# Single products as fillers, a top-64 split around the first dots, and picks that alternate with attention queries

## The reference, cut to what matters

```python
h = rmsnorm(x, ln1_g)
q_a, k_a, v_a, q_i, k_i, w_i, q_b, k_b, v_b, g_b = project(h, w_in)

# sparse attention: an indexer scores all keys, the top 64 (132 for the streams) are attended to
dots = einsum('bthd,bsd->bths', q_i, k_i)
score = where(allowed, einsum('bth,bths->bts', w_i, relu(dots)), -inf)
top_s, idx = lax.top_k(score, topk)
o_a = attention over the rows idx of k_a, v_a
# retention: a chunkwise recurrence with a state per head
x = x + concat([o_a, o_b]) @ w_out

# PEER: per token and head, 16 of 128 x 128 experts; an expert is one row of peer_u and one of peer_v
h = rmsnorm(x, ln2_g)
q = h @ w_query                        # 8 heads, two halves of 128
v1, i1 = top_k(q[first half] @ keys1.T, 16); v2, i2 = top_k(q[second half] @ keys2.T, 16)
cand_s = v1[:, None] + v2[None, :];  top_s, sel = top_k(cand_s, 16);  gate = softmax(top_s)
act = gelu(einsum('thkd,td->thk', peer_u[e_idx], h))
x = x + einsum('thk,thkd->td', gate * act, peer_v[e_idx])
y = rmsnorm(x, ln_final_g)
```

## Time and profile before

| | |
|---|---|
| median of 3 runs | 1145.67 us (1145.54 to 1146.6) |
| profiled execution | 1144.68 us, of which span 1142.9 us |
| PE busy | 858.6 us (75%) |
| DVE busy | 784.3 us (69%) |
| POOL busy | 539.9 us (47%) |
| ACT busy | 453.6 us (40%) |
| moved by DMA | 456.60 MB, of which the gathers' queue 402.68 MB |

### The profile page before, as it was taken

One profiled execution on the slowest core, in us unless ns is written; L12 is line 12 of the kernel. 1 busy time (PEld: TensorE's weight loads), 2 busy tenths in 40 slices (PEclk: granted clock), 3 DMA queues, 4 the chain that ended last, 5 costly groups with the idle time before them and its releaser, 6 DMA issues.

```text
span 1142.9 us, 12079 instructions
## 1 busy us (share of the span) xinstructions
PE 858.6 (75%) x3879; PEld 396.1 (35%) x3884; DVE 784.3 (69%) x2005; ACT 453.6 (40%) x1423; POOL 539.9 (47%) x437
## 2 busy tenths in 40 slices
PE   8999988997896858685586777576766675656566
PEld 6748743443232424242243342133223222211111
DVE  2325877876677778986666786757877767667544
ACT  2121444333443434543564663343343333333334
POOL 0002444553555645563553554555564555465452
PEclk9999999999998988998888998799788779887869
DMA  9902999999999999999999999999999999999996
GB/s 375 410 2 73 418 425 426 426 425 429 426 402 424 426 429 426 425 401 415 425 427 425 425 427 428 419 427 427 426 426 427 427 426 428 427 426 428 427 427 274
DMA packets 66791, 456.60 MB, mean 400 GB/s; under 512 B 8227, under 2 KB 10019, under 8 KB 15526
## 3 DMA queue, kind: packets, MB, share of 16 engines
q0 software_dynamic: 55888, 402.68, 83.8%
q1 hardware_dynamic: 10694, 52.87, 11.5%
q10 hardware_dynamic: 144, 0.26, 0.1%
HBM read 451.49 MB, written 3.24 MB: 398 GB/s over the span
## 4 chain that ended last, share of the span: by engine, by line
DMA 45%; PE 29%; DVE 13%; POOL 5%; ACT 4%; issue 4%; SPq 0%; POOLq 0%; DVEq 0%
DMA rows<-in_uv,ids 32%; PE ps L598 28%; DMA wt<-in_uv,ids 9%; DVE rows L2042 6%; POOL rows L537 2%; POOL work L520 1%; DMA rows<-in_w_qi 1%; DMA wt<-in_uv,last_ids 1%; DVE wt L2042 1%; ACT wt L1249 1%; ACT work L1249 1%; DMA wt<-in_w_q 1%; ACT wgt L1249 1%; POOL wt L537 1%; PE ps L601 1%
## 5 line engine op out<-in xcount | busy, mean ns | idle before, releaser
L537 POOL DMA_INDIRECT rows<-in_uv,ids x352 | 401.8, 1141 | 439.2 <-PE ps L598 355.4
L598 PE MATMUL ps<-rows,work 128*64 128x512 f32 x1416 | 409.1, 706 | 240.9 <-ACT work L1249 240.5
L2042 DVE CUSTOM_DVE_ANT_0 rows<-rows,wt 128x1024 f32<-128x1024 f32 x226 | 276.7, 1225 | 162.3 <-DMA rows<-in_uv,ids 161.0
L1249 ACT ACTIVATE zact<-zdot 128x1 f32<-128x1 f32 x354 | 71.4, 202 | 485.7 <-DVE zdot L2042 485.1
L598 PEld LDWEIGHTS ps<-rows,work 128*64 128x64 f32 x1416 | 95.9, 151 | 471.8 <-ACT work L1249 333.8
L598 PE MATMUL ps<-wt 128*128 128x128 f32 (+6 forms) x719 | 198.4, 484 | 31.0 <-ACT wt L1249 29.5
L2042 DVE CUSTOM_DVE_ANT_0 rows<-rows,masks 128x1024 f32<-128x1024 f32 x128 | 156.2, 1223 | 67.9 <-DMA rows<-in_uv,ids 66.9
L598 PEld LDWEIGHTS ps<-wt 128*128 128x128 f32 (+2 forms) x724 | 98.8, 188 | 111.0 <-issue 62.1
L1249 ACT ACTIVATE work<-pair,wgt 128x64 f32<-128x64 f32 x354 | 123.1, 348 | 11.6
L1249 ACT ACTIVATE wgt<-zact,gates 128x1 f32<-128x1 f32 x354 | 104.3, 295 | 11.5
L598 PEld LDWEIGHTS ps<-work,wt 128*128 128x128 f32 (+1 forms) x664 | 82.5, 198 | 50.4 <-issue 49.9
(11 more groups left out here) (178 smaller groups left out, 722.9 us busy)
## 6 DMA issues: line engine op xcount, KB each, us to landing
wt<-in_w_q SPq DMA_DIRECT2D x7, 2048.0 KB, 12.0
rows<-in_uv,ids POOLq DMA_INDIRECT x352, 14.3
rows<-in_w_out SPq DMA_DIRECT2D x2, 2048.0 KB, 32.7
wt<-in_w_out SPq DMA_DIRECT2D x2, 2048.0 KB, 12.0
wt<-in_ckv SPq DMA_DIRECT2D x16, 256.0 KB, 11.6
x<-in_x SPq DMA_DIRECT2D x5, 512.0 KB, 8.3
rows<-in_w_qi SPq DMA_DIRECT2D x1, 2048.0 KB, 13.1
wt<-in_w_qa SPq DMA_DIRECT2D x1, 2048.0 KB, 13.1
```

What stands on the lines that cost most here:

```text
L537: pool.indirect_dma_start(row[s], None, a["uv"], bass.IndirectOffsetOnAxis(ap=ids[:, own(n // KP).start + n % KP:own(n // KP).start + n % ...
L598: return nc.tensor.matmul(out, lhsT, rhs, start=start, stop=stop)
L1249: return nc.scalar.activation(*args, **kw)
L2042: V.tensor_tensor_reduce(row[s][:, 0:D], row[s][:, 0:D], h2r[t][:, n % 2, :], 1.0, 0.0, ALU.mult, ALU.add, zdots[s]).then_inc(dotted, 1)
```

## The change

- `index_queries` takes its range in single products (32 of them) and not in blocks of 8, and its calls among the opening's steps are cut finer: 3, 4 and 2 products where 8, 8 and 8 were, and 4 of tile 2 ahead of `dots_1` where 8 were; what is left of each comes later.
- The transposes of tile 0's normed tokens go in two halves (`h2_t0`), each as soon as its half of the columns is there. The wait for ACT's sum of squares moves from PE to the two copies behind the transposes.
- `spread_out(0)` goes ahead of `dots_1(3)`.
- `y_start(0)` moves from before the first add to tick 12. The first add clears its accumulator itself (start flag), and `y_start(0)` adds to it.
- The first four pairs of picks alternate with the four `later_qa` on PE; `query_scores(1)` stands ahead of them. On ACT picks 6 and 7 come ahead of the second copy.
- Of tile 1's eight rounds of top-64, DVE does four before the first dot and the others, one a tick, behind the first dots. Tile 1's attention moves back by 1 to 6 ticks.

```diff
-            index_queries(1, 6, 0, 1)
-            h2_t(0)
-            index_queries(1, 6, 1, 2)
+            h2_t0(0)
+            index_queries(1, 6, 0, 3)
+            h2_t0(1)
+            index_queries(1, 6, 3, 7)
             query(0)
-            index_queries(1, 6, 2, 3)
+            index_queries(1, 6, 7, 9)
             query_scores(0)
-            index_queries(1, 6, 3, 4)
+            index_queries(1, 6, 9, 32)
             pe.wait_ge(gb_sb, 1)
-            index_queries(2, 7, 0, 1)
+            index_queries(2, 7, 0, 4)
...
             sums_1(0)
+            spread_out(0)
             dots_1(3)
             sums_1(1)
-            spread_out(0)
             sums_1(2)
             sums_1(3)
-            index_queries(2, 7, 1, 4)
+            index_queries(2, 7, 4, 32)
             query(1)
-            later_qa(0)
             query_scores(1)
             pe.wait_ge(qi_sb, 3)
-            y_start(0)
             add_experts(0)
+            later_qa(0)
+            add_experts(2)
             later_qa(1)
-            add_experts(2)
+            add_experts(4)
             pe.wait_ge(scored, 2)
             later_qa(2)
+            add_experts(6)
             later_qa(3)
-            add_experts(4)
```

PE, the new transposes and tile 1's attention; `until` counts picks:

```diff
+            def h2_t0(e):
+                pe.wait_ge(gained, e + 1)
+                for c in range(4 * e, 4 * e + 4):
+                    last = tr(ps[:, 3 * e, (c % 4) * P:(c % 4 + 1) * P], h2[:, c * P:(c + 1) * P])
+                if e:
+                    last.then_inc(h2t_ps, 1)
...
             def attention_1():
+                yield from until(6)
                 scores_1(0)
-                yield from until(6)
+                yield from until(8)
                 scores_1(1)
-                yield from until(14)
+                yield from until(12)
+                y_start(0)
+                yield from until(16)
                 prob_t1(0)
```

ACT, the copies of the attention queries among the first picks:

```diff
             for n in range(4):
                 weigh(n)
             later_qa(0)
-            for n in range(4, 6):
+            for n in range(4, 8):
                 weigh(n)
             later_qa(1)
             for n in range(UNITS * KP):
...
-                if n > 5:
+                if n > 7:
                     weigh(n)
```

DVE, the rounds:

```diff
-            for r in range(0, TOPK[1], 8):
+            for r in range(0, TOPK[1] // 2, 8):
                 whole(score_round(score1, r, TOPK[1], 0))
                 whole(score_round(score1, r, TOPK[1], 1))
-            set_bias(bias1, score1)
...
             def attention_1():
-                yield from until(8)
+                for r in range(TOPK[1] // 2, TOPK[1], 8):
+                    whole(score_round(score1, r, TOPK[1], 0))
+                    yield from score_round(score1, r, TOPK[1], 1)
+                set_bias(bias1, score1)
+                yield from until(10)
```

More of the change, by code:

```diff
@@ L628, in keys_values, with index_queries @@
                 natural(t, w_kv, 6 + t % 2, NKV).then_inc(kv_ps, 1)
[L630 to L635, removed]
+            def index_queries(t, bank, i0, i1):
+                for i in range(i0, i1):
+                    j, c = divmod(i, KC)
+                    last = mm(ps[:, bank, j * P:(j + 1) * P], w_qi[:, c, j * P:(j + 1) * P], hT(t, c), c == 0, c == KC - 1)
+                if i1 == 4 * KC:
                     last.then_inc(qi_ps, 1)
@@ L646, in _ @@
             pe.wait_ge(w_in["qi"], 16)
-            index_queries(0, 4, 0, 2)
+            index_queries(0, 4, 0, 16)
             norm_t(1)
-            index_queries(0, 4, 2, 3)
+            index_queries(0, 4, 16, 24)
             norm_t(2)
-            index_queries(0, 4, 3, 4)
+            index_queries(0, 4, 24, 32)
             keys_values(1)
@@ L787, in scores_1 @@
                 last.then_inc(sc_ps, 1)
-            def h2_t(t):
[L790 to L794, removed]
+            def h2_t0(e):
[4 more added lines that the diff above has]
+                    last.then_inc(h2t_ps, 1)
+            def h2_t(t):
+                pe.wait_ge(hready, TILES + t + 1)
                 if t == 1:
@@ L866, in y_start @@
                 for e in range(2):
-                    last = mm(ps[:, Y_BANK[t] + e, :], ident[:], x[:, t, e * 512:(e + 1) * 512], True, False)
+                    last = mm(ps[:, Y_BANK[t] + e, :], ident[:], x[:, t, e * 512:(e + 1) * 512], t > 0, False)
                 last.then_inc(y_init, 1)
@@ L880, in add_experts @@
                         s = ring(n + j)[0]
-                        last = mm(ps[64 * j:64 * j + 64, Y_BANK[n // (HP * KP)] + e, :], diag[s], row[s][:, D + e * 512:D + (e + 1) * 512], False, stop)
+                        last = mm(ps[64 * j:64 * j + 64, Y_BANK[n // (HP * KP)] + e, :], diag[s], row[s][:, D + e * 512:D + (e + 1) * 512], n == 0, stop)
                 last.then_inc(acc, 1)
@@ L1145, in attention_1 @@
             def attention_1():
+                yield from until(6)
                 scores_1(0)
-                yield from until(6)
+                yield from until(8)
                 scores_1(1)
-                yield from until(14)
+                yield from until(12)
+                y_start(0)
+                yield from until(16)
                 prob_t1(0)
-                yield from until(18)
+                yield from until(20)
                 values_1(0)
                 prob_t1(1)
-                yield from until(22)
+                yield from until(24)
                 values_1(1)
@@ L1241, in _ @@
                     y_start(n // (HP * KP))
-                if n > 4:
+                if n > 6:
                     add_experts(n, n % (HP * KP) == HP * KP - 2)
@@ L1311, in h2_take @@
                 act.wait_ge(h2t_ps, t + 1)
+                if t == 0:
+                    act.wait_ge(sqd, H2_STAT[0] + 1)
                 if t > 0:
@@ L1437, in background @@
             def background():
-                yield from until(11)
+                yield from until(13)
                 exps_1(0)
                 exps_1(1)
-                yield from until(19)
+                yield from until(21)
                 prob_t1(0)
-                yield from until(22)
+                yield from until(24)
                 values_1(0)
                 prob_t1(1)
-                yield from until(25)
+                yield from until(27)
                 values_1(1)
@@ L1718, in h2_take @@
                 dve.wait_ge(h2t_ps, t + 1)
+                if t == 0:
+                    dve.wait_ge(sqd, H2_STAT[0] + 1)
                 if t > 0:
@@ L1897, in attention_1 @@
             def attention_1():
-                yield from until(8)
+                for r in range(TOPK[1] // 2, TOPK[1], 8):
[3 more added lines that the diff above has]
+                yield from until(10)
                 yield from row_max(1, [ps[:, b, :].rearrange("p (j n) -> p j n", j=2) for b in (1, 2)], 0, 4)
-                yield from until(10)
+                yield from until(12)
                 yield from row_max(2, [ps[:, b, :].rearrange("p (j n) -> p j n", j=2) for b in (0, 3)], 4, 4)
-                yield from until(15)
+                yield from until(17)
                 yield from scale_probs(1, prob1[:, 0, :, :], 0, 4)
```

## The result

The changed kernel took 1157.53 us (median of four runs, 1156.15 to 1158.3) against 1145.91 for the kernel before in the same comparison. The ratio is 1.0101, interval 1.0088 to 1.0114: slower by 1%, 11.6 us. The profiled execution took 1158.21 us (span 1156.2), 13.5 more than that of before.

A forecast was written before the change was run, and what follows sets the result against it. The prediction took the DMA stream of rows and weights as the bound from about 111 us. Dry gaps of 10.0 us less 2.8 of earlier start gave 1145.67 + 7.2 = 1152.9 us, whole range 1146.5 to 1158.

The forecast's parts named there:

- the lead: Opening, up to gather 0: fewer fillers and earlier transposes start the gather stream 2.8 us earlier, at 106.6.
- the split: Tile 1's top-64 rounds on DVE: moving four behind the first dots changes 0 us (from -1 to +0.5).
- add 0: PE's first add, of picks 0 and 1: runs from 123.9 to 125.7, letting gather 8 go at 126.0.
- wait ahead of add 4: Add of picks 4 and 5: PE stands still 2.4 us for ACT, whose copy waits for the second attention query.
- gather 12: Issued at 139.5 behind add 4, bringing bytes at 141.1: stream dry for 1.9 us.
- gather 18: Issued at 166.0 behind query 2 and add 10, bringing bytes at 167.6: stream dry for 6.3 us.
- The load, taken at its old 10.1 us: SP's 2 MB weight load, issued at 148.3: query 2 starts at 158.4, after a 5.7 us PE wait.
- forecast of +7.2: Whole program: 10.0 us of dry stream less 2.8 of earlier beginning, chance 0.5.
- the rival of the slow short queue: Gathers 12, 13, 18, 19 and 20, running nearly alone, move a quarter slower: 4 us more, 1157, chance 0.15.
- rule on turns between rings: DMA engines alternate between rings by packet: the load lands sooner beside few gathers, the sum 3 us less.
- The rival in which the load comes in time: Load lands 5 us after its bytes begin, query 2 at 155.4, 3 dry us go: 1148 to 1150, chance 0.2.
- The kept gain: Front's gain survives if gather 12 is issued by 137.6 and gather 18 by 159.7: -2.8, 1142.9, chance 0.12.

The follow-up runs named there:

- e2: Only the new order of first adds and attention queries, moved y_start and later tile 1 attention, on the kernel before: ratio 1.0092, 1156.32 us.
- e1: Only the opening's edits (single-product fillers, transposes in halves, earlier spread) on the kernel before: ratio 1.0011, 1146.75 us.
- e3: Only the split of tile 1's top-64 rounds, on the kernel before: ratio 1.0003.
- e4: Changed kernel plus products into an unused PSUM bank during PE's three waits: 1154.52 us, ratio 1.0083 to the kernel before.
- e6: Changed kernel with unit 2's query one pair of picks later: 1152.61 us, ratio 1.0065 to the kernel before.
- e5: Changed kernel with ACT's first copy of the attention queries behind the weighs of picks 4 and 5: 1156.62 us, ratio 1.0096 to the kernel before.
- e7: Changed kernel with the edits of e5 and e6 together: 1151.71 us, ratio 1.0046 to the kernel before.
- e9: As e8, with the add of picks 4 and 5 moved behind attention query 2: 1146.44 us, ratio 1.0003 to the kernel before.
- e10: As e9 but without e6's edit, unit 2's query at its old tick: 1149.38 us, ratio 1.0036 to the kernel before.
- e8: As e7, with attention query 0 ahead of unit 1's scores and the first two adds together: 1147.19 us, ratio 1.0012 to the kernel before.

## Why the prediction was right

The forecast was 1152.9 in a range of 1146.5 to 1158; 1157.53 lies in it, near its end. The mechanism held at every place of PE's chain, and the runs confirm its parts: the picks' order alone makes the loss (e2), the lead is worth nothing (e1, e2), the split alone is worth nothing (e3).

| step | forecast | profile after |
|---|---|---|
| gather 0 | 106.6 | 107.03 |
| add 0 starts | 123.9 | 123.84 |
| wait ahead of add 4 | 2.4 | 2.34 |
| gather 12 | 139.5 | 142.80 |
| weight load issued | 148.3 | 151.69 |
| query 2 starts | 158.4 | 163.14 |
| gather 18 | 166.0 | 172.02 |
| gather 20 | 172.1 | 178.10 |

Up to add 0 all agrees. From there two terms are missing or small, and together they are the difference of 6.0 us:

- The granted clock, which the working doesn't have. PE's rows behind its three waits are longer by 0.5 (add 0), 1.2 (attention query 0), 1.6 (add 4) and 1.4 (query 2), 4.7 in all; the first three alone are the 3.3 us by which gather 12 is late. With the clock kept at 1.00 (e4) gather 20 goes at 173.3, 1.2 behind the forecast. I read the clock as 1.00 up to 200 us in the kernel before and took that for the new one too, though the working gave PE waits of some 2.5, 2.4 and 5.7 us where it had had at most 1.1 before the load's query.
- The load, taken at its old 10.1 us, needed 11.4 (and 10.4 to 12.4 in the experiments).

7.2 + 6.0 is 13.2, and the spans differ by 13.3. The medians differ by 11.6 only. In e2 and e6 the first two waits (2.34 and 2.35 us) left the clock at 1.00, in e5 and e7 the first brought it down, so the runs that were not profiled may have paid less; that is argued, not shown. In the median the forecast of +7.2 is 4.4 short, and the time lies only 0.5 inside the range's end: that it is inside at all is owed to the room left for the rivals, and is luck as far as these two terms go.

The lead was 2.4 and not 2.8: the spread started at 106.02 and not 105.6, the top 16 at 95.86 and not 95.7. It did not matter, since after the first hole PE's chain and not the stream's beginning set the time. The stream's side of the sum was off too: gathers 0 to 11 were done near 141.2 and not at 139.2, and gathers 12 and 18 brought bytes some 2 us after their issue and not 1.6.

Since PE's chain sets the time, the rival of the slow short queue, true in some rows (377 GB/s from 132 to 140), is no term of its own here: a gather that moves slowly ahead of a hole only narrows the hole. That its 1157 stands beside the measured 1157.5 is chance. In e1, which has no hole, slow rates are what takes the lead back. But the length of the queue doesn't give the rate: by an estimate from issues and bytes moved, 0.3 to 2.3 gathers were outstanding in that stretch, yet the kernel before moved 427 GB/s from 126 to 140 with 0.8 to 3.4, and the changed one 419 from 123 to 132 with 1.2 to 2.8. The 320 GB/s that the rival took from the earlier trace rows include the stream's first microsecond at 156; the four behind it moved 360.

The Trainium skill's rule on turns between rings (DMA: Bandwidth & Descriptors, Queues, rings and completion order) was weighed to make the load faster beside a short queue. It took longer instead. The forecast said that the trace agrees with the rule, since the load took twice the time of its bytes; the bytes by queue don't show that. In the kernel before the load's queue moved 0.03 MB in the first 2 us behind its issue, and 1.62 MB in the next 4, in which the gathers got 0.16, though gathers 12 and 13 had been issued. In the changed kernel, with an estimated 1.9 MB of gathers outstanding at its issue for 1.0 before, the load moved nothing for 3 us and then 0.15 to 0.43 MB a microsecond, while the gathers fell from 0.32 to 0.02. So the bytes queued before the load go first, and then the load takes most of the rate. The delay alone doesn't give the time: e6, with the same 3 us, needed 10.4 in all and e5 12.4. What sets the rest, and the rates below 426, stays open.

The rival in which the load comes in time fell with its 11.4 us. The kept gain fell at gather 12, which its own condition put at 137.6.

## What to carry to other kernels

When a stream is the bound, look for the moment at which everything issued has landed. A transfer that happens to cover that moment belongs to the schedule: moving what releases it, here by two more adds ahead of the last attention query, opens a hole that no earlier start pays for. In every queue that is in order, check what stands behind each new wait, the copy on ACT and the query on PE here. And where a new order gives TensorE waits like these (2.3 and 7.2 us), price the work behind them at both clock levels.

## What the runs showed of the hardware

- The granted clock fell from 1.00 to 0.50 (2.4 to 1.2 GHz) with waits of 2.34, 2.34 and 7.20 us in the changed kernel: in the add behind the first wait, at the end of the second, within the third. Some 3 us of PE's work ran at the lower clock each time. Products into an unused bank during the waits kept it at 1.00 (e4). Waits of 2.34 and 2.35 us left it at 1.00 in e2 and e6. The Trainium skill (TensorE: Matmul & The Clock Gate, Part 1) says that the counter behind the gate runs freely, so that the same kernel can meet it in different phases. The changed kernel and e6, whose PE order is the same up to the add of picks 8 and 9, fit that: the same two waits brought the clock down in one and not in the other. There is one profile of each kernel.
- The stream moved 342 GB/s (e1, 130 to 140 us) and 377 (changed kernel, 132 to 140) at DMA shares of 0.95 and 0.98, with an estimated 0.7 to 2.4 and 0.3 to 2.3 gathers of 1.05 MB outstanding. With 0.8 to 3.4 it moved 427 in the kernel before (126 to 140).
- A 2 MB load beside gathers needed 10.1 to 12.4 us from its issue to the start of its first user. It brought no bytes for the first 3 us where 1.6 MB or more of gathers were outstanding at its issue (estimate; changed kernel, e2, e4 to e7, e9, e10), and after 1 to 2 us where 0.6 to 1.0 MB were (kernel before, e1, e3, e8).
